# Second block's two output gates in three passes from split slabs, queries' norm applied in the logits' copies, recurrence gates and short keys moved up

## Chip, core and metric

One core of a Trainium2 chip runs the whole program, a stack of three model blocks on 256 tokens of width 1024, in one launch. The metric is the device time of one execution in microseconds (us). Each core has a matrix engine (TensorE; in rows PE for its matmuls, PEld for its weight loads, clock 1.2 or 2.4 GHz), VectorE (DVE), ScalarE (ACT), GpSimd (POOL) and SyncE (SP), which issues the large loads. Matmul results land in eight PSUM banks. Each engine runs its own instructions in the order in which they are written and waits on semaphores for the others.

## What is computed

The change lies in the second block's mixer. Cut to it, with `s` = 256 tokens, 8 heads of 128, 2 key and value heads, 8 index heads of 64:

```python
xn = _rmsnorm(x, mix_norm); h = xn @ w_in          # w_in: 1024 x 6216
lru_x, lru_gate, q, k, v, qi, ki, wi, gate_a, gate_b = _split_cols(h)
ua = _causal_dwconv(lru_x, ...)                    # width 4
r = sigmoid(ua @ wa + ba); i = sigmoid(ua @ wx + bx)     # 8 blocks of 128
log_a = -8 * r * softplus(-lam); a = exp(log_a)
u = sqrt(-expm1(2 * log_a)) * (i * ua)
h_t = a_t * h_(t-1) + u_t                          # over the 256 tokens
ya = (h * gelu(lru_gate)) @ w_lru_br
qh = _rmsnorm(q per head, q_norm); kh = _rmsnorm(k per head, k_norm)
score = sum_h wi_h * relu(qi_h . ki / 8)           # causal; top 64 keys for each token
probs = softmax(qh . kh / sqrt(128) + bias[bucket(dist)])   # over these 64
yb = (probs @ v) @ w_attn_br
merged = sigmoid(gate_a) * ya + sigmoid(gate_b) * yb
x = x + merged @ w_out
```

The first block (a mixer and 16 experts) runs ahead of it, and this block's feed-forward part and a third block of two layers behind it. All is in float32.

## The kernel before

**Products.** The activations `h` of the second block stand feature-major (feature on the partition, 256 tokens along the row) in three forms: whole in `hT`, and as a rounded high part and the rest, `h2_high` and `h2_low`. `feature_major` (products at L1039) multiplies a whole float32 slab of weights by the whole activations. `feature_major3` splits each weight slab too: ACT's `high` (L1855) writes the rounded high part to a spare area, DVE's `low` (L2366) writes the rest over the slab, and `mm3` (L968, L969, L970) adds three products: high x high, high x low, low x high. A slab is 1024 x 512 weights, 2 MB; `high` and `low` work on it in two halves of 128 x 2048. A product of 128 x 256 has 32 places in a slab (4 groups of output features, 8 chunks of the 1024).

**Loads and banks.** Slabs go through a ring of three places. SP issues the load of a slab when TensorE has finished the slab three before it (`load`, L751). Results take the four work banks in turn (`open_bank`); TensorE may fill a bank only when the result that it held four batches before has been copied out, mostly by ACT (`copied`, `frees`).

**Order on TensorE around the change.** Slabs `lru_x`, `lru_x1`, `lru_gate`, `q`, `kv`; five sums of squares with `ones_mean` (`qk_ms`, L1367), four for the queries, one for the keys; slab `qi`; the recurrence's gates (`lru_ri`, L1376); the short keys and index weights (`kiwi`, L1380); slabs `gate_a` (whole, L1039); eight index score batches (`indexer`, L1400), two ahead of slab `gate_b` 0 and six within it; `gate_b` (whole); the logits (L1420); the slabs `lru_out` 0 and 1; transposes of the softmax (L1430 to L1432).

**Order on DVE.** `low` of `qi`; five reciprocals (L2771) and products (L2772) that norm queries and keys in place; the recurrence (L2778 to L2785, scan L2787) with ACT's tanh (L2024), exp (L2027) and square root (L2034) between; its product with the gelu gate in two parts (`u_high`, `u_low`, L2793 to L2796); the index scores (L2807, L2809), whose `relu` copies ACT makes; mask (L2816); eight rounds of maximum and replacement for tokens 0 to 127 (L2822, L2823); `low` of `lru_out` 0; eight rounds for tokens 128 to 255; threshold, bias and row maximum of the logits (L2829 to L2846); `low` of `lru_out` 1; the softmax's division. The order on each engine is written out by hand, and nothing reorders it.

## Time and profile before

| | us |
|---|---|
| median of three runs | 2667.01 |
| lowest, highest | 2665.62, 2667.71 |
| the profiled execution's own time | 2669.58 |
| its span, first to last instruction | 2667.8 |
| TensorE busy, share of the span | 2319.9, 87% |
| VectorE busy | 1345.1, 50% |
| ScalarE busy | 808.8, 30% |

The profile is of one execution. Its rows give times from the start of the span. TensorE's busy time counts overlapping matmuls once; how fast it goes is read from the distance of their starts. A row of the timeline merges neighbours of one line and shape and gives, in brackets, the idle time before it and who ended it. The stretch that the change touches begins at about 1190 us and ends at about 1376 us. What lies behind it is reached in the same order by both kernels.

### The profile page before, as it was taken

Reading aid. Unit: us, or ns where it says so; the run is one execution under the profiler, and the core shown is the slowest. Engines: PE = TensorE matmul, PEld = TensorE weight load, DVE = VectorE, ACT = ScalarE, POOL = GpSimd, SP = SyncE. Lnnn points to the kernel's source line nnn. Section 1 sums busy time; section 2 is a strip of 40 time slices with the busy share of each in tenths; the row PEclk is TensorE's granted clock in tenths of the full one; section 3 lists DMA queues with packets and bytes.
Section 4 is the critical chain, followed back from the end, with each engine's and each line's share of the span. In section 5 each row is a group of like instructions: output and inputs, shape, how many; then the busy total and the mean of one; then the engine's idle time right before and its main releaser. Section 6 shows DMA issues by size and latency. Waiting matters only on the chain.

```text
span 2667.8 us, 34798 instructions
## 1 busy us (share of the span) xinstructions
PE 2319.9 (87%) x14416; PEld 1695.4 (64%) x14416; DVE 1345.1 (50%) x1894; ACT 808.8 (30%) x1141; POOL 22.9 (1%) x41
## 2 busy tenths in 40 slices
PE   6999767666766676689999999999999999999999
PEld 5997222112211222149898998888968888887887
DVE  5865100000000000035687776877687778777776
ACT  3342000000000000024454334434574334345433
POOL 1000000000000000000000000000000000000000
PEclk9999887887788878899999999999999999999999
DMA  9948999999999999985445555555505555552553
GB/s 386 355 171 345 398 428 428 428 428 428 428 428 429 429 429 428 428 353 186 165 144 172 189 189 174 178 191 183 187 5 184 191 176 191 189 178 82 183 189 127
DMA packets 219734, 720.23 MB, mean 270 GB/s; under 512 B 8312, under 2 KB 126088, under 8 KB 191600
## 3 DMA queue, kind: packets, MB, share of 16 engines
q1 hardware_dynamic: 217632, 708.87, 68.6%
q0 software_dynamic: 2000, 9.91, 1.0%
q8 instruction: 75, 1.23, 0.2%
q14 instruction: 27, 0.22, 0.0%
HBM read 717.68 MB, written 3.16 MB: 270 GB/s over the span
## 4 chain that ended last, share of the span: by engine, by line
PE 64%; DMA 30%; DVE 3%; SPq 1%; issue 1%; ACT 1%; POOLq 0%; POOL 0%; DVEq 0%; ACTq 0%
PE bank L1494 12%; DMA AB<-in_w_up_e 8%; PE bank L968 6%; PE bank L1496 6%; PE bank L970 6%; PE bank L969 6%; DMA AB<-in_w_gate_e 5%; DMA AB<-in_w_down_e 5%; PE bank_pair L968 5%; PE bank_pair L969 5%; PE bank_pair L970 5%; DMA HT<-in_w_up_e 4%; DMA HT<-in_w_gate_e 3%; DMA HT<-in_w_down_e 3%; PE bank L1274 2%; PE bank L1039 2%
## 5 line engine op out<-in xcount | busy, mean ns | idle before, releaser
L1496 PEld LDWEIGHTS bank<-HT_r,ring_r 128*128 128x128 f32 x1408 | 265.3, 188 | 62.3
L2665 DVE TENSOR_TENSOR A<-bank,A 128x512 f32<-128x512 f32 x16 | 11.1, 692 | 580.6 <-PE bank L1274 580.6
L1496 PE MATMUL bank<-HT_r,ring_r 128*128 128x256 f32 x1408 | 277.3, 278 | 0.0
L970 PE MATMUL bank<-HT_r,ring_r 128*128 128x256 f32 x904 | 255.9, 283 | 0.0
L2366 DVE TENSOR_TENSOR ring_r<-ring,AB_r 128x2048 fp32r<-128x2048 f32 (+1 forms) x81 | 179.9, 2261 | 51.1 <-ACT AB_r L1855 50.0
L1494 PE MATMUL bank<-HT_r,AB_r 128*128 128x512 f32 x640 | 203.2, 399 | 2.2 <-DVE HT_r L2374 2.2
L1494 PE MATMUL bank<-HT_r,AC_r 128*128 128x512 f32 x640 | 201.0, 395 | 0.0
L2366 DVE TENSOR_TENSOR ring_r<-ring,AC_r 128x2048 fp32r<-128x2048 f32 x66 | 148.4, 2289 | 73.8 <-ACT AC_r L1855 73.7
L2366 DVE TENSOR_TENSOR ring_r<-ring,A_r 128x2048 fp32r<-128x2048 f32 (+1 forms) x80 | 171.6, 2179 | 27.1 <-ACT A_r L1855 27.1
L2092 ACT ACTIVATE XB<-XB 128x256 f32<-128x256 f32 x112 | 46.8, 418 | 436.4 <-DVE XB L2935 320.6
L1274 PE MATMUL bank<-ring,A 128*32 128x512 f32 x768 | 116.2, 732 | 70.6 <-DMA ring<-in_w_up_e 47.6
L969 PE MATMUL bank_pair<-ring_r,XA_r 128*128 128x512 f32 x448 | 174.5, 389 | 0.0
L970 PEld LDWEIGHTS bank<-HT_r,ring_r 128*128 128x128 f32 x904 | 173.5, 192 | 0.0
L1855 ACT ACTIVATE AB_r<-ring 128x2048 fp32r<-128x2048 f32 (+1 forms) x79 | 145.0, 1883 | 57.2 <-PE bank L970 15.9
L970 PE MATMUL bank_pair<-A_r,XB_r 128*128 128x512 f32 x408 | 158.8, 389 | 0.0
L1956 ACT ACTIVATE A<-bank 128x512 f32<-128x512 f32 x16 | 9.6, 597 | 489.4 <-PE bank L1274 489.4
L2407 DVE TENSOR_REDUCE XB<-bank 128x256 f32<-128x512 f32 x176 | 120.8, 686 | 62.4 <-PE bank L1496 62.4
L968 PE MATMUL bank_pair<-A_r,XA_r 128*128 128x512 f32 x384 | 149.6, 390 | 0.0
L1855 ACT ACTIVATE AC_r<-ring 128x2048 fp32r<-128x2048 f32 x66 | 123.2, 1915 | 84.7 <-DMA ring<-in_ffn_w_gu 74.0
L1855 ACT ACTIVATE A_r<-ring 128x2048 fp32r<-128x2048 f32 (+1 forms) x80 | 142.2, 1816 | 12.9 <-DMA ring<-in_w_out 11.4
L1814 ACT ACTIVATE A<-bank 128x256 f32<-128x256 f32 (+2 forms) x56 | 22.7, 413 | 400.7 <-PE bank L1283 298.1
L969 PE MATMUL bank<-HT_r,AB_r 128*128 128x256 f32 x488 | 138.1, 283 | 0.0
(579 smaller groups left out, 4697.1 us busy)
## 6 DMA issues: line engine op xcount, KB each, us to landing
ring<-in_ffn_w_gu SPq DMA_DIRECT2D x88, 1024.0 KB, 6.7
ring<-in_w_gate_e SPq DMA_DIRECT2D x24, 2048.0 KB, 35.8
ring<-in_w_up_e SPq DMA_DIRECT2D x24, 2048.0 KB, 32.2
ring<-in_w_in SPq DMA_DIRECT2D x46, 1024.0 KB, 10.2
ring<-in_w_down_e SPq DMA_DIRECT2D x23, 2048.0 KB, 36.9
ring<-in_ffn_w_down SPq DMA_DIRECT2D x40, 1024.0 KB, 6.2
ring<-in_w_up SPq DMA_DIRECT2D x24, 1024.0 KB, 6.6
A<-in_w_ada SPq DMA_DIRECT2D x17, 1024.0 KB, 11.6
```

Source lines behind the costliest of these rows:

```text
L968: mm(out_, lhs[0], rhs[0], start=start, stop=False, skip_group_check=True)
L969: mm(out_, lhs[0], rhs[1], start=False, stop=False, skip_group_check=True)
L970: return mm(out_, lhs[1], rhs[0], start=False, stop=stop, skip_group_check=True)
L1039: last = mm(b[:, f * T:(f + 1) * T], w[:, at:at + P], src[:, k, :], start=(k == 0), stop=(k == n_k - 1))
L1274: last = mm(b[32 * j:32 * j + 32, :], xe_now[:, k, :], w[:, col0:col0 + 512], start=(k == 0), stop=(k == DC - 1), tile_position=(0, 32 * j ...
L1494: mm(both, high, h_both[:, :, k, :], start=(k == 0), stop=False, skip_group_check=True)
L1496: last = mm(both[:, 1, :], lows[k - k0], h_high[:, k, :], start=False, stop=(k == DC - 1), skip_group_check=True)
L1814: frees(run(dst, work_bank(name, i)[0:rows_, 0:n], ACT.Copy, scale=scale), name, i)
L1855: run(area[:, :], w[:, at:at + area.shape[1]], ACT.Copy).then_inc(S["high_ready"], 1)
L2092: run(f_act[b % 2], f_conv[b % 2], fn).then_inc(S["gelu_done"], 1)
L2366: v.tensor_tensor(twins[f"ring{slot}"][:, part], ring[slot][:, part], area[:, :].bitcast(fp32), ALU.subtract).then_inc(S["low_ready"], 1)
L2407: frees(v.tensor_reduce(dst, both, AX.X, ALU.add), name, i)
```

## The change

Both gates' slabs are loaded as two halves of 256 output features each and go through `high`, `low` and `mm3`, one half (one work bank, two groups of features) at a time. `high_half` on ACT and `low(..., which=...)` on DVE are placed one by one among the other work. The areas for the high halves are ones that are free at that point: a half's area is reused when the batches that read it are done. For the queries, 16 products with one column of `ones_mean` give the mean squares of each token and head as a column; `q_scale` is their root's reciprocal times 1/sqrt(128), and ACT multiplies by it when it copies the logits (16 copies of one head instead of 8 of two). Both norms' gains go into the keys (`gain_qk`). `kiwi` and `lru_ri` stand ahead of `qi` on TensorE, and the slab of `lru_ri` ahead of that of `qi` in the ring. The bias for the later tokens is loaded as two halves into other places, straight after the table that it is read from. `u_high` lies elsewhere.

```diff
@@ -253,14 +253,14 @@
     p.add("lru_gate", "WWWW", [1, 3], split=2)
     p.add("q", "WWWW", [1, 3], split=2)
     p.add("kv", "WW", [1], split=1)
-    p.add("qk_ms", "W" * 5)
+    p.add("qk_ms", "WW")
+    p.add("kiwi", "W")
+    p.add("lru_ri", "W" * 8, [7])
     p.add("qi", "WW", [1], split=1)
-    p.add("lru_ri", "W" * 8, [7])
-    p.add("kiwi", "W")
-    p.add("gate_a", "WWWW", [1, 3])
+    p.add("gate_a", "WWWW", [1, 3], split=2)
     p.add("wi", "W")
     p.add("score", "AA")
-    p.add("gate_b", "AAWAAAAWWW", [7, 9])
+    p.add("gate_b", "AAWAAAAWWW", [7, 9], split=2)
     p.add("logits2", "W" * 8)
...
-    bias2_last = AB[:, 2048:4096].rearrange("p (h s) -> p h s", h=8)
+    bias2_last = [a.rearrange("p (h s) -> p h s", h=4)
+                  for a in (const("dft_seq"), row("gate_f"))]
+    q_scale, gain_qk = narrow(16), narrow(1)
     bias_row = A[3][0:8, 1024:1536]
     relu_s = [A[6][:, at:at + 512].rearrange("p (d s) -> p d s", d=2) for at in (0, 512)]
     score = A[6][:, 1024:1536].rearrange("p (t s) -> p t s", t=TT)
...
     h_high, h_low = h_both[:, 0, :, :], h_both[:, 1, :, :]
-    u_high, u_low = fm(twins["AB"][:, 0:2048]), fm(twins["AC"][:, 0:2048])
+    u_high, u_low = fm(twins["HT"][:, 2048:4096]), fm(twins["AC"][:, 0:2048])
     h2_high, h2_low = fm(twins["AB"][:, 0:2048]), fm(twins["AB"][:, 2048:4096])
     hid_high = twins["A8"][:, 0:1536].rearrange("p (f t) -> p f t", t=T)
     hid_low = twins["A0"][:, 0:1536].rearrange("p (f t) -> p f t", t=T)
...
         t_ = {n: twins[n][:, :] for n in ("AB", "A3", "A4", "A5", "A6", "A8")}
-        if name in ("lru_x1", "lru_gate", "q", "kv", "qi"):
+        xn_r = twins["xn"][:, :, :].rearrange("p t d -> p (t d)")
+        if name == "qi":
+            return [(0, xn_r), (2048, t_["A6"])]
+        if name in ("gate_a", "gate_b"):
+            ht, a0 = twins["HT"][:, 2048:4096], twins["A0"][:, :]
+            a, b = {("gate_a", 0): (ht, xn_r), ("gate_a", 1): (t_["A6"], t_["A4"]),
+                    ("gate_b", 0): (a0, xn_r), ("gate_b", 1): (t_["A4"], xn_r)}[name, s]
+            return [(0, a), (2048, b)]
+        if name in ("lru_x1", "lru_gate", "q", "kv"):
             if (plan.split0[name] + s - plan.split0["lru_x1"]) % 2 == 0:
                 return [(0, twins["AC"][:, 2048:4096]), (2048, t_["A4"])]
             return [(0, t_["A3"]), (2048, twins["xn"][:, :, :].rearrange("p t d -> p (t d)"))]
         if name in ("lru_out", "attn_out"):
-            xn_r = twins["xn"][:, :, :].rearrange("p t d -> p (t d)")
             ht_0, ht_1 = twins["HT"][:, 0:2048], twins["HT"][:, 2048:4096]
...
@@ -866,13 +875,15 @@
         dense("lru_gate", w_in2, 2, 1024)
         dense("q", w_in2, 2, 2048)
         dense("kv", w_in2, 1, 3072)
-        dense("qi", w_in2, 1, 3584)
         sl = slot("lru_ri", 0)
         gate_w = [dram(n).rearrange("(b c) d -> c b d", c=P) for n in ("lru_wa_2", "lru_wx_2")]
         load("lru_ri", 0, [(ring[sl][:, i * D:(i + 1) * D].rearrange("p (b d) -> p b d", b=8), gate_w[i])
                            for i in range(2)])
-        dense("gate_a", w_in2, 2, 4168)
-        dense("gate_b", w_in2, 2, 5192)
+        dense("qi", w_in2, 1, 3584)
+        for name, c0 in (("gate_a", 4168), ("gate_b", 5192)):
+            for s in range(2):
+                dst = ring[slot(name, s)][:, :].rearrange("p (a k n) -> p a k n", a=2, k=8)
+                load(name, s, [(dst[:, a, :, :], k_rows(w_in2, c0 + 512 * s + 256 * a, 256)) for a in range(2)])
...
-        for i in range(5):
-            b = open_bank("qk_ms", i)
-            src = sq2[:, 2 * i:2 * i + 2, :].rearrange("p c t -> p (c t)") if i < 4 else sqk[:, :]
-            batch(mm(b[:, :], ones_mean[:, :], src, start=True, stop=True))
-        feature_major3("qi", 0, 0, h2_parts)
+        b = open_bank("qk_ms", 0)
+        for t in range(TT):
+            for h in range(8):
+                last = mm(b[:, 8 * t + h:8 * t + h + 1], sq2[:, h, t * P:(t + 1) * P], ones_mean[:, 0:1],
+                          start=True, stop=True)
+        batch(last)
+        b = open_bank("qk_ms", 1)
+        batch(mm(b[:, :], ones_mean[:, :], sqk[:, :], start=True, stop=True))
+        b = open_bank("kiwi", 0)
+        for k in range(DC):
+            last = mm(b[0:72, 0:T], w_kiwi[:, k, :], hT[:, k, :], start=(k == 0), stop=(k == DC - 1))
+        batch(last)
         pe.wait_ge(S["ua_ready"], 1)
         w = slab("lru_ri", 0)
         for i in range(8):
@@ -1375,12 +1393,25 @@
                 at = (i // 4) * D + n * P
                 last = mm(b[:, j * T:(j + 1) * T], w[:, at:at + P], l_ua[:, n, :], start=True, stop=True)
             batch(last)
-        b = open_bank("kiwi", 0)
-        for k in range(DC):
-            last = mm(b[0:72, 0:T], w_kiwi[:, k, :], hT[:, k, :], start=(k == 0), stop=(k == DC - 1))
-        batch(last)
+        feature_major3("qi", 0, 0, h2_parts)
+
+        def gate3_slab(name, s, batches, behind=None):
+
+            w = split_slab(name, s)
+            for g in range(2):
+                b = open_bank(name, batches[g])
+                for f in range(2):
+                    for k in range(DC):
+                        last = mm3(b[:, f * T:(f + 1) * T], w(2048 * g + 256 * k + f * P, P), h2_parts(k),
+                                   k == 0, k == DC - 1)
+                    if behind and f == 0:
+                        behind(2 * g)
+                batch(last)
+                if behind:
+                    behind(2 * g + 1)
+
         for s in range(2):
-            feature_major("gate_a", 2 * s, s, hT, DC)
+            gate3_slab("gate_a", s, (2 * s, 2 * s + 1))
         copied(pe, "kiwi", 0)
         b = open_bank("wi", 0)
         for t in range(TT):
@@ -1409,9 +1440,9 @@
 
         indexer(0)
         indexer(1)
-        feature_major("gate_b", 0, 0, hT, DC, behind=indexer_pair, batches=GATE_B_AT[0:2])
-        feature_major("gate_b", 0, 1, hT, DC, batches=GATE_B_AT[2:4])
-        pe.wait_ge(S["qk_ready"], 5)
+        gate3_slab("gate_b", 0, GATE_B_AT[0:2], behind=indexer_pair)
+        gate3_slab("gate_b", 1, GATE_B_AT[2:4])
+        pe.wait_ge(S["qk_ready"], 2)
         for t in range(TT):
...
+            w = loaded(act, name, s)
+            at, area = halves(name, s)[half]
+            run(area[:, :], w[:, at:at + area.shape[1]], ACT.Copy).then_inc(S["high_ready"], 1)
+
         filled(act, "kv", 0)
         run(k2[:, :, :].rearrange("p g t -> p (g t)"), work_bank("kv", 0)[:, :], ACT.Copy)
         frees(run(sqk[:, :], work_bank("kv", 0)[:, :], ACT.Square), "kv", 0)
         copy_out("kv", 1, v2[:, :, :].rearrange("p t n -> p (t n)"))
 
-        for i in range(5):
-            filled(act, "qk_ms", i)
-            frees(run(root[i][:, :], work_bank("qk_ms", i)[:, :], ACT.Sqrt, bias=eps_col[:, 0:1]), "qk_ms", i)
+        high_half("qi", 0, 0)
+        filled(act, "qk_ms", 0)
+        frees(run(q_scale, work_bank("qk_ms", 0)[:, 0:16], ACT.Sqrt, bias=eps_col[:, 0:1]), "qk_ms", 0)
+        filled(act, "qk_ms", 1)
+        frees(run(root_k[:, :], work_bank("qk_ms", 1)[:, :], ACT.Sqrt, bias=eps_col[:, 0:1]), "qk_ms", 1)
+        high_half("qi", 0, 1)
+        filled(act, "kiwi", 0)
+        for d in range(2):
+            run(ki[64 * d:64 * d + 64, :], work_bank("kiwi", 0)[0:64, 0:T], ACT.Copy)
+        frees(run(wi_rows, work_bank("kiwi", 0)[64:72, 0:T], ACT.Copy), "kiwi", 0)
+        high_half("gate_a", 0, 0)
 
         def ri(i):
 
@@ -2013,8 +2057,6 @@
             two("lru_ri", i, lambda f, b: run(dst[:, 2 * (i % 4) + f, :], b, ACT.Sigmoid,
                                               bias=col(bias, 2 * (i % 4) + f)))
 
-        for i in range(2):
-            copy_out("qi", i, qi[:, 2 * i:2 * i + 2, :].rearrange("p g t -> p (g t)"))
         for i in range(8):
             ri(i)
         for i in range(4):
...
-            run(ki[64 * d:64 * d + 64, :], work_bank("kiwi", 0)[0:64, 0:T], ACT.Copy)
-        frees(run(wi_rows, work_bank("kiwi", 0)[64:72, 0:T], ACT.Copy), "kiwi", 0)
+        for i in range(2):
+            copy_out("qi", i, qi[:, 2 * i:2 * i + 2, :].rearrange("p g t -> p (g t)"))
+        high_half("gate_a", 0, 1)
+        high_half("gate_a", 1, 0)
         act.wait_ge(S["mult_in"], 1)
         run(l_t[:, :, :], l_t[:, :, :], ACT.Sqrt).then_inc(S["mult_out"], 1)
+        high_half("gate_a", 1, 1)
         act.wait_ge(S["scan_done"], 1)
+        high_half("gate_b", 0, 0)
         for i in range(4):
             filled(act, "gate_a", i)
             frees(run(l_a[:, 2 * i:2 * i + 2, :].rearrange("p g t -> p (g t)"), work_bank("gate_a", i)[:, :],
                       ACT.Sigmoid), "gate_a", i)
+            if i == 1:
+                high_half("gate_b", 0, 1)
```

Left out are lines on views and areas, the logits' copies on ACT (described above), POOL's two loads of the bias in place of one, and the placement of `low` on DVE, which the pieces below and this list give: `qi` half 0 ahead of the roots' reciprocals, `qi` half 1 and `gate_a` 0 half 0 behind them; `gate_a` 0 half 1 behind the product that ACT's square root waits for; both halves of `gate_a` 1 ahead of the scan; `gate_b` 0 half 0 behind the scan's first product with the gelu gate, half 1 behind `u_low`; `gate_b` 1 half 0 between the fourth and fifth index score, half 1 behind the eighth.

**ScalarE from the values' copy to the first sigmoid of the recurrence.** Before (L1814 the values' copy and the copies of `qi`, L2008 the roots, L2013 the sigmoids):

```order
L1814 ACTIVATE A<-bank 128x512 [waits products_done]
L2008 ACT_TABLE_LOAD
L2008 ACTIVATE XA<-bank,eps_col 128x512 [waits products_done] x4
L2008 ACTIVATE XB<-bank,eps_col 128x512 [waits products_done]
L1814 ACTIVATE A<-bank 128x512 [waits products_done] x2
L2013 ACT_TABLE_LOAD
L2013 ACTIVATE AC<-bank,cols 128x256 [waits products_done]
```

Now (L1845 the values' copy, L2035 a high half, L2044 and L2046 the roots, L2050 and L2051 the short keys, L2057 the sigmoids):

```order
L1845 ACTIVATE A<-bank 128x512 [waits products_done]
L2035 ACTIVATE XA_r<-ring 128x2048 [waits slab_loaded0]
L2044 ACT_TABLE_LOAD
L2044 ACTIVATE small<-bank,eps_col 128x16 [waits products_done]
L2046 ACTIVATE XB<-bank,eps_col 128x512 [waits products_done]
L2035 ACTIVATE A_r<-ring 128x2048 [waits slab_loaded0]
L2050 ACTIVATE XB<-bank 64x256 [waits products_done]
L2050 ACTIVATE XB<-bank 64x256
L2051 ACTIVATE XB<-bank 8x256
L2035 ACTIVATE HT_r<-ring 128x2048 [waits slab_loaded1]
L2057 ACT_TABLE_LOAD
L2057 ACTIVATE AC<-bank,cols 128x256 [waits products_done]
```

Both halves of `qi` and the first of `gate_a` stand ahead of the first sigmoid; the copies of `qi` have gone behind the recurrence's exp.

**VectorE at the end of the index scores.** Before:

```order
L2809 SCALAR_TENSOR_TENSOR A<-A,small 128x256 [waits relu_done,relu_used]
L2809 SCALAR_TENSOR_TENSOR A<-A,small 128x256 [waits dve_own]
L2816 TENSOR_TENSOR A<-A,masks 128x128 [waits relu_used]
L2816 TENSOR_TENSOR A<-A,masks 128x256
L2822 MAX small<-A 128x8 [waits dve_own]
```

Now:

```order
L2874 SCALAR_TENSOR_TENSOR A<-A,small 128x256 [waits relu_done,relu_used]
L2874 SCALAR_TENSOR_TENSOR A<-A,small 128x256 [waits dve_own]
L2420 TENSOR_TENSOR ring_r<-ring,XA_r 128x2048 [waits high_ready,relu_used]
L2882 TENSOR_TENSOR A<-A,masks 128x128
L2882 TENSOR_TENSOR A<-A,masks 128x256
L2888 MAX small<-A 128x8 [waits dve_own]
```

The last low half of `gate_b` stands between the scores and the mask, and it waits for ACT's high half.

**ScalarE from the sixth to eighth index score to the logits' copies.** Now (L2094 relu, L2035 a high half, L2106 the sigmoids of `gate_b`, L2115 the logits' copies):

```order
L2094 ACTIVATE A<-bank_pair 128x512 [waits relu_used,products_done] x4
L2035 ACTIVATE XA_r<-ring 128x2048 [waits slab_loaded1,products_done]
L2106 ACTIVATE A<-bank 128x512 [waits products_done] x2
L2035 ACTIVATE XB_r<-ring 128x2048 [waits slab_loaded2]
L2106 ACTIVATE A<-bank 128x512 [waits products_done] x2
L2035 ACTIVATE XA_r<-ring 128x2048 [waits slab_loaded2]
L2115 ACTIVATE A<-bank,small 128x128 [waits products_done,qk_ready]
```

Before, both halves of `lru_out` 0 stood between the second and the third sigmoid. Now the second of them stands behind the fourth, and the first L2035 row, the last half of `gate_b`, waits until TensorE has done with slab `gate_b` 0, whose high half lay in the same area.

## Rows read from the trace of the kernel before

**Rows 1.** Chain that ended last: start us, us, what; 1281 to 1366

```profile
1286.07 27.63 PE bank L1039 x128
...
1328.22 0.61 ACT A L2048
...
1331.00 0.64 DVE A L2816 x2
...
1337.40 4.49 DVE ring_r L2366 x2
1341.89 0.35 DVE small L2822
...
1361.46 4.41 DVE ring_r L2366 x2
...
1365.92 0.39 PE bank L968
```

**Rows 2.** Timeline of TensorE: start us, us, engine, line, operation, count, idle before

```profile
1190.18 0.47 PE L968 MATMUL bank<-AB_r,AC_r 128*128 128x256 f32 x1
...
1259.74 3.60 PE L1367 MATMUL bank<-A,ones_mean 128*128 128x512 f32 x8
...
1275.54 7.07 PE L1376 MATMUL bank<-AC,ring 128*128 128x256 f32 x32
1282.45 3.62 PE L1380 MATMUL bank<-HT,w_kiwi 128*72 128x256 f32 x16
1285.90 27.79 PE L1039 MATMUL bank<-HT,ring 128*128 128x256 f32 x128
1313.62 0.61 PE L1387 MATMUL bank<-consts,XB 8*128 8x8 f32 x4
...
1345.90 5.40 PE L1420 MATMUL bank<-A,HT 128*128 128x128 f32 x32
...
1350.95 0.47 PE L968 MATMUL bank<-AB_r,XA_r 128*128 128x256 f32 x1
...
1363.71 0.39 PE L968 MATMUL bank<-AB_r,HT_r 128*128 128x256 f32 x1 [0.91 <-DVE ring_r L2366]
...
1365.92 0.39 PE L968 MATMUL bank<-AB_r,HT_r 128*128 128x256 f32 x1 [0.50 <-DVE ring_r L2366]
```

**Rows 3.** Timeline of TensorE, 20 to 36 us: a restart, narrow products

```profile
20.57 8.04 PE L1103 MATMUL bank<-ones 128*128 128x512 f32 x12 [20.57 <-DVE XB L2423]
...
32.02 3.63 PE L1113 MATMUL bank<-ones,XB 128*128 128x1 f32 x32
```

**Rows 4.** Timeline of ScalarE, 1249 to 1298 us

```profile
1249.39 1.92 ACT L1855 ACTIVATE AC_r<-ring 128x2048 fp32r<-128x2048 f32 x1
1251.20 1.91 ACT L1855 ACTIVATE A_r<-ring 128x2048 fp32r<-128x2048 f32 x1
...
1276.36 1.28 ACT L2013 ACT_TABLE_LOAD   x1
1277.65 3.03 ACT L2013 ACTIVATE AC<-bank,cols 128x256 f32<-128x256 f32 x8
...
1283.38 3.38 ACT L2024 ACTIVATE XB<-AC,small 128x256 f32<-128x256 f32 x8
```

**Rows 5.** Timeline of VectorE, 1266 to 1316 us

```profile
1266.62 3.35 DVE L2771 RECIPROCAL XA<-XA 128x512 f32<-128x512 f32 x1
1270.01 0.75 DVE L2772 SCALAR_TENSOR_TENSOR HT<-HT,cols,XA 128x512 f32<-128x512 f32 x1
...
1300.40 4.77 DVE L2787 TENSOR_TENSOR_SCAN AC<-AC,A 128x256 f32<-128x256 f32 x8
...
1315.19 0.29 DVE L2807 TENSOR_SCALAR A<-A,small 128x128 f32<-128x128 f32 x1 [3.17 <-ACT A L2048]
```

**Rows 6.** Windows: us, busy PE, PEld, DVE, ACT, POOL, PEclk, DMA share, GB/s

```profile
1939.50:1942.20 2.70, 0.06 (x1) 0.00 (x0) 2.56 (x8) 0.00 (x0) 0.00 (x0) 1.00 0.00 0
...
1945.00:1946.00 1.00, 1.00 (x8) 0.39 (x4) 0.84 (x4) 1.00 (x6) 0.00 (x0) 0.50 0.00 0
```

## What was predicted

> **What bounds the kernel now.** I read the chain of waits first, then each engine's timeline in the stretch that is changed. The chain [rows 1] runs through TensorE while it works on `gate_a` (128 matmul records in 27.63 us) and through the index scores up to 1328; then it leaves TensorE: ACT's relu, DVE's mask at 1331.00, its rounds of maximum and replacement, `low` of `lru_out` 0 among them at 1337.40, and `low` of `lru_out` 1 at 1361.46. TensorE comes back at 1365.92. The reader is to see in [rows 2] that TensorE has work without a gap up to 1363.71 and then waits 0.91 and 0.50 us for DVE: from the scores on, DVE ends last, and TensorE is only 1.4 us less late. So time taken from TensorE ahead of `lru_out` 1 comes through only as far as it brings DVE's scores forward, and each microsecond that DVE gains or loses between 1331 and 1366 is one of the kernel.
>
> **Price on TensorE.** Six slabs in three passes take from 1190.18 to 1259.74, 11.6 us each; the two whole slabs of `gate_a` take from 1285.90 to 1313.62, 13.9 us each [rows 2]. Four slabs gain 4 x 2.3 = 9.1 us. The queries' sums: 16 narrow products have the form of the 32 records in 3.63 us [rows 3], against 8 of the 10 records up to 1263.2, 3.4 us: nothing. The logits' count is the same. So at most 9 us are there.
>
> **Price on the others.** A high half costs ACT 1.8 us from start to start [rows 4], a low half DVE 2.2 us (4.49 for two) [rows 1]; eight of each are added, 14.5 and 17.6 us. DVE loses four reciprocals and four products, 4 x 4.1 = 16.4 us [rows 5], but ahead of the recurrence, while seven of the eight low halves stand behind the recurrence's exp. I follow the three engines from 1259.7, each operation with its length in these rows.
>
> *Up to the recurrence.* TensorE: 3.5 for the queries, 0.8 for the keys, 3.4 for `kiwi` (1282.45 to 1285.90) [rows 2]: the recurrence's gates begin at 1267.5 instead of 1275.54. They need four work banks; the fifth batch waits for ACT's first sigmoid. ACT has in front of that sigmoid three high halves, the copies of roots and short keys and two table loads of 1.28 [rows 4]: values' copy to 1260.5, high half 1262.3, table 1263.6, roots 1264.8, high half 1266.6, short keys (they are ready at 1267.6) 1268.9, high half 1270.7, table 1272.0. TensorE stands from 1271.0 to 1272.8 and ends the gates at 1276.3, `qi` at 1287.9.
>
> *Recurrence.* Sigmoids to 1278.1 (before 1283.4), tanh 3.1, table 1.3, exp 3.3: 1285.8; two operations of 2.3 on DVE: 1290.4. ACT must first wait for `qi`'s second batch at 1287.9, copy it and make two high halves, so the square root ends at 1295.4 instead of 1298.0. DVE: product 2.3, two low halves 4.4, scan 4.8 [rows 5]: 1306.9, where before it was 1305.2. The five microseconds won at the sigmoids are gone. TensorE gets the low halves of `gate_a` just in time (one wait of 0.6 for the third half) and ends `gate_a` at 1311.7 (before 1313.6).
>
> *Scores.* DVE: `u_high`, low, product, `u_low`, low, 5 x 2.2: first score at 1318.0 instead of 1315.19 [rows 5]. TensorE runs `gate_b` 0 with six score batches between 1312.8 and 1327.5, 11.6 + 2.4 for the scores + 0.6 for waits. Four scores of 0.8, a low half 2.2, four of 1.0 and a wait of 0.7 end DVE's scores at 1328.0; the mask began at 1331.00 before [rows 1]: 3 us ahead.
>
> *The two new waits.* Now the last low half of `gate_b` stands ahead of the mask. ACT can make its high half only when TensorE has done `gate_b` 0, 1327.5 + 1.9 = 1329.4; DVE then needs 2.3: mask at 1331.7. Behind DVE's waiting instruction the mask, all rounds and `low` of both `lru_out` slabs are queued. The same sum made for the kernel before gives 1330.6 where the row says 1331.0, so I count the difference of sums, +1.1. The second: `low` of `lru_out` 0 half 1. ACT makes its high half behind the last sigmoid of `gate_b`, at 1339.1 + 0.5 + 1.9 = 1341.5; DVE would be there at 1340.3: +1.3. The bias added as two operations for the later tokens: +0.15. Small hand-overs that the sums miss by some tenths for each round trip between TensorE and ACT: +0.15. Together DVE hands over `low` of `lru_out` 1 **2.7 us later**. Without either wait it would be 0.2 us earlier; with `gate_b` ending 1 us later than I put it, 3.7 later. These are the bounds.
>
> *What becomes of TensorE's gain.* The logits go from 1338.9 to 1345.6 (ACT begins to copy them at 1341.5, a wait of 1.5; they were at 1345.90 to 1350.95) [rows 2], `lru_out` 0 ends at 1357.3, and then TensorE stands until about 1366: 8.5 us, the 9 us that it was to gain.
>
> *The clock.* An idle stretch of 2.7 us [rows 6] is followed by a granted clock of 0.50, which is 1.2 GHz, in the third microsecond of work behind it. After 20.57 us of idle 12 records of 128x512 take 8.04 us [rows 3], where such a record takes 0.43 at full clock (twice the 27.63 / 128 of a record of 256 columns) [rows 1]: 2.9 us lost. So behind 8.5 us of idle `lru_out` 1 begins at half clock. Nearest rows: 2.9 lost at the most, nothing at the least (the slab behind the waits of 0.91 and 0.50 shows no loss); of what is lost 0.6 lies in the wait for the second low half, which TensorE no longer reaches early. I take 1.5, in the upper half, as both idle rows show the drop. The Trainium skill ("TensorE: Matmul & The Clock Gate", Part 1) says that the throttled clock is the default and that activity releases it. By that rule work after a long wait always pays; the trace agrees [rows 3, 6].
>
> *Strict order.* DVE does no instruction ahead of one that waits; the chain in [rows 1] shows its rounds and `low` strictly in written order. The Trainium skill ("TensorE: Matmul & The Clock Gate", Architectural detail) says that ScalarE and VectorE are strict FIFO, while TensorE may pull weight loads ahead. It speaks against this change: if DVE could pass the waiting low half, the sum would be 1.1 less.
>
> *Moved and hidden.* The bias for the later tokens is loaded ahead of the queries' slabs instead of behind `qi`; its reader stands behind the threshold, far later in both. `lru_ri` and `qi` change places in the ring; each has over 10 us to land. Slabs of the gates are released later than needed by none: high halves are asked for more than 6 us after each release. If `gate_a` 0 lands after 1268.9, ACT's sigmoids go with it, microsecond for microsecond. 16 logits' copies instead of 8 cost ACT some 1.4 us more; they are done at 1346.8, and DVE asks for them at 1352.8.
>
> **Sum.** +2.7 + 1.5 = +4.2 us. The profiled execution took 2669.58 and would take 2673.8. It lies 2.6 above the median of the runs shown, so the median goes from 2667.0 to **2671.2**.
>
> **Rivals.**
>
> *The clock falls twice (slower than 0.2%).* TensorE also stands 1.8 us at the fifth gate batch. If the clock falls there too, up to 1.7 us are lost in `qi`; the high halves that wait for `qi` and `gate_b` shift by it, and both new waits grow. At a shift of 1.3 the time is 2671.2 + 1.3 = 2672.5; from 1.2 on it is over the bound. For it: [rows 6] fell after 2.7. Against it: no loss behind the 0.91 [rows 2], and nothing in between is measured in dense work. A clock loss of 2.9 instead of 1.5 gives the same.
>
> *The waits don't bind (no change).* If ACT's high halves come earlier than summed, DVE is 0.2 early, TensorE idles 6, and the clock costs 1.5: 2668.3.
>
> *The gain arrives (faster).* If DVE had slack that the chain hides, the 9.1 us would show: 2658. Against it stand the two waits for DVE in [rows 2].
>
> **How the numbers follow.** The forecast has 0.53, the clock twice or longer 0.27, no binding waits 0.13, the full gain 0.07. A change under 0.2%, 5.3 us, can't be told from none here. Faster needs under 2661.7: 0.07. Slower needs over 2672.3: 0.27. The same: 0.66. For 8 in 10 the range leaves out the full gain and the far end of the clock: 2665.5 (DVE 0.2 early, no clock loss, runs 1 us apart) to 2674.5 (3.7 + 2.9 + 0.9 for the runs).
>
> **What the changed profile would show.** TensorE idle for 8 to 9 us ahead of `lru_out` 1, ended by DVE; a granted clock of half for some microseconds behind it; DVE waiting about 1 us for ACT ahead of the last `gate_b` half and of the second `lru_out` 0 half; `gate_a` ending near 1311.7, the mask near 1332, transposes of the softmax some 4 us after 1376. I am wrong if DVE reaches the mask before 1330, or if TensorE's wait ahead of `lru_out` 1 is under 4 us.

## The result, and the profile after

| | before | after |
|---|---|---|
| median of 17 runs each, us | 2668.07 | 2675.32 |
| lowest, highest | 2664.16, 2670.17 | 2665.94, 2677.14 |
| span of the profiled execution | 2667.8 | 2675.3 |

The ratio is 1.0026, with a 95% interval from 1.002 to 1.0032: the changed kernel is slower by 0.26%, some 7 us. The forecast was 2671.2 and its range ended at 2674.5, so both were too low.

The page of the changed kernel, busy time of each engine:

```profile
PE 2331.0 (87%) x14568; PEld 1704.1 (64%) x14568; DVE 1347.8 (50%) x1898; ACT 822.9 (31%) x1154; POOL 23.5 (1%) x42
```

TensorE is busy for 11 us more than before, though four slabs now take 11.6 us instead of 13.9. All of it lies in the experts, ahead of the changed part (568.6 us busy between 300 and 1150, before 555.9), where the loads set the time: the sum of busy time says nothing on this change. TensorE's timeline in the changed kernel (start, us, engine, line, operation, count, idle time before and who ended it); it answers to [rows 2]:

```profile
1189.72 0.47 PE L979 MATMUL bank<-AB_r,AC_r 128*128 128x256 f32 x1
...
1259.27 4.26 PE L1378 MATMUL bank<-ones_mean,A 128*128 128x1 f32 x32
1263.38 2.05 PE L1382 MATMUL bank<-XB,ones_mean 128*128 128x512 f32 x2
1265.23 5.44 PE L1385 MATMUL bank<-HT,w_kiwi 128*72 128x256 f32 x16
1270.51 3.62 PE L1394 MATMUL bank<-AC,ring 128*128 128x256 f32 x16
1276.00 1.78 PE L1394 MATMUL bank<-AC,ring 128*128 128x256 f32 x7 [1.87 <-ACT AC L2057]
...
1315.10 0.61 PE L1418 MATMUL bank<-consts,XB 8*128 8x8 f32 x4
...
1345.91 3.72 PE L1451 MATMUL bank<-A,HT 128*128 128x256 f32 x16 [1.21 <-ACT A L2115]
...
1369.55 0.58 PE L979 MATMUL bank<-HT_r,AB_r 128*128 128x256 f32 x1 [8.42 <-DVE ring_r L2420]
...
1383.42 0.27 PE L1461 MATMUL bank<-consts,A 128*128 128x128 f32 x1
```

The wait of 8.42 us ahead of `lru_out` 1 is there, as forecast. Two rows are not as forecast: the short keys' 16 records take 5.44 us where they took 3.62 [rows 2], and the 32 narrow records take 4.26 where 32 of that form took 3.63 [rows 3]. No idle time stands ahead of either. The windows say why (us, busy time of PE, PEld, DVE, ACT, POOL, then the granted clock, DMA share, GB/s). Kernel before:

```profile
1262.50:1268.90 6.40, 6.40 (x45) 5.45 (x45) 6.30 (x3) 2.42 (x5) 0.00 (x0) 1.00 0.73 274
```

Changed kernel:

```profile
1262.50:1268.90 6.40, 6.40 (x16) 3.79 (x17) 4.79 (x5) 3.42 (x4) 0.00 (x0) 0.50 0.76 248
...
1361.10:1364.50 3.40, 0.03 (x1) 0.00 (x0) 3.37 (x3) 2.51 (x14) 0.00 (x0) 1.00 0.61 183
1364.50:1369.50 5.00, 0.00 (x0) 0.00 (x0) 4.97 (x4) 2.17 (x9) 0.00 (x0) 0.50 0.78 295
1369.50:1374.60 5.10, 5.05 (x23) 5.05 (x24) 5.03 (x5) 5.10 (x10) 0.00 (x0) 0.50 0.02 3
```

The clock was granted at half (1.2 GHz) twice. The second time is behind the long wait, from 1364.5 to 1374.7. The first time TensorE was busy without a gap: the clock fell at 1262.1, 2.8 us after the narrow sums began, and stayed at half for 6.8 us, through the keys' sum and most of the short keys.

VectorE in the changed kernel, the halves ahead of the mask and of `lru_out`:

```profile
1321.39 0.28 DVE L2872 TENSOR_SCALAR A<-A,small 128x128 f32<-128x128 f32 x1
...
1333.82 2.29 DVE L2420 TENSOR_TENSOR ring_r<-ring,XA_r 128x2048 fp32r<-128x2048 f32 x1 [2.40 <-ACT XA_r L2035]
1336.03 0.62 DVE L2882 TENSOR_TENSOR A<-A,masks 128x128 f32<-128x128 f32 x2
...
1345.38 2.29 DVE L2420 TENSOR_TENSOR ring_r<-ring,XA_r 128x2048 fp32r<-128x2048 f32 x1 [0.66 <-ACT XA_r L2035]
...
1367.21 2.28 DVE L2420 TENSOR_TENSOR ring_r<-ring,AB_r 128x2048 fp32r<-128x2048 f32 x1
```

ScalarE, the high half for which the mask waits; TensorE's end of `gate_b` 0 lets it start:

```profile
1331.43 1.91 ACT L2035 ACTIVATE XA_r<-ring 128x2048 fp32r<-128x2048 f32 x1 [1.40 <-PE bank L981]
```

**Measuring by the stretch.** The first product in three passes behind the experts begins at 1190.18 before and at 1189.72 after; over all profiles of this study it begins anywhere from 1183.4 to 1190.2, and what follows the transposes takes 1287.8 to 1293.2 (one run apart, below). These differences lie outside the changed part. So kernels are compared by the time from that first product to the first transposes of the softmax, "the stretch": 185.91 us before, 193.70 after, +7.79. The rest takes 1291.7 before and 1291.9 after. The stretch falls into four pieces:

| piece | forecast | measured |
|---|---|---|
| end of `gate_a` on TensorE | -1.9 | +1.94 (123.44 to 125.38) |
| from there to the mask on DVE | +3.0 | +3.55 (17.38 to 20.93) |
| from there to `low` of `lru_out` 1 | +1.6 | +0.80 (30.38 to 31.18) |
| from there to the transposes (clock) | +1.5 | +1.50 (14.71 to 16.21) |
| sum | +4.2 | +7.79 |

### The profile page after: what moved, and what is told of

Same layout as the page of the kernel before. It is cut to its first block, busy times and chain, and to the rows that moved or that the text cites. A ratio compares the mean times of both kernels' runs of the same rounds, so it can differ in the third digit from the quotient of the medians.

```text
span 2675.3 us, 35104 instructions
## 1 busy us (share of the span) xinstructions
PE 2331.0 (87%) x14568; PEld 1704.1 (64%) x14568; DVE 1347.8 (50%) x1898; ACT 822.9 (31%) x1154; POOL 23.5 (1%) x42
## 4 chain that ended last, share of the span: by engine, by line
PE 63%; DMA 31%; DVE 3%; ACT 1%; SPq 1%; issue 1%; POOLq 0%; POOL 0%; DVEq 0%; ACTq 0%
PE bank L1525 12%; DMA AB<-in_w_up_e 11%; DMA AB<-in_w_gate_e 9%; DMA AB<-in_w_down_e 9%; PE bank L979 7%; PE bank L980 7%; PE bank L981 7%; PE bank L1527 6%; PE bank_pair L979 5%; PE bank_pair L980 5%; PE bank_pair L981 5%; PE bank L1285 2%; PE bank L1320 1%; DMA A<-in_w_ada 1%; SPq L760 1%
## 5 line engine op out<-in xcount | busy, mean ns | idle before, releaser
L1527 PEld LDWEIGHTS bank<-HT_r,ring_r 128*128 128x128 f32 x1408 | 265.3, 188 | 62.4
L1527 PE MATMUL bank<-HT_r,ring_r 128*128 128x256 f32 x1408 | 277.3, 278 | 0.0
L981 PE MATMUL bank<-HT_r,ring_r 128*128 128x256 f32 x968 | 274.8, 284 | 0.0
L2420 DVE TENSOR_TENSOR ring_r<-ring,A_r 128x2048 fp32r<-128x2048 f32 (+1 forms) x83 | 178.4, 2183 | 28.3 <-ACT A_r L1886 27.5
L981 PEld LDWEIGHTS bank<-HT_r,ring_r 128*128 128x128 f32 x968 | 186.8, 193 | 0.0
L2420 DVE TENSOR_TENSOR ring_r<-ring,AC_r 128x2048 fp32r<-128x2048 f32 x65 | 146.2, 2288 | 69.5 <-ACT AC_r L1886 69.4
L1845 ACT ACTIVATE A<-bank 128x256 f32<-128x256 f32 (+2 forms) x56 | 22.9, 413 | 392.5 <-PE bank L1294 295.6
## 6 DMA issues: line engine op xcount, KB each, us to landing
A<-in_w_ada SPq DMA_DIRECT2D x17, 1024.0 KB, 11.6
```

Of the source, the lines that this page charges most:

```text
L981: return mm(out_, lhs[1], rhs[0], start=False, stop=stop, skip_group_check=True)
L1527: last = mm(both[:, 1, :], lows[k - k0], h_high[:, k, :], start=False, stop=(k == DC - 1), skip_group_check=True)
L2420: v.tensor_tensor(twins[f"ring{slot}"][:, part], ring[slot][:, part], area[:, :].bitcast(fp32), ALU.subtract).then_inc(S["low_ready"], 1)
```

## The experiments

All kernels in one table. `gate_a` ends and stretch are of one profiled execution each; the last two columns are of the timed runs, each group of kernels with runs of the kernel before on the same chip. The edits below are given in short form. "At half behind the sums": whether the clock was granted at half in the 15 us from 69.5 us on in the stretch.

| kernel | at half behind the sums | `gate_a` ends | stretch | median | ratio to before, interval |
|---|---|---|---|---|---|
| before | no | 123.44 | 185.91 | | |
| after | yes | 125.38 | 193.70 | 2675.32 | 1.0026 (1.002 to 1.0032) |
| after_again | yes | 125.38 | 193.79 | 2672.46 | 1.0023 (1.0009 to 1.0037) |
| a1_wide_sums | yes | 125.39 | 193.70 | 2670.97 | 1.0009 (0.9999 to 1.0019) |
| a5_interleaved | no | 126.18 | 194.24 | 2674.12 | 1.0032 (1.0022 to 1.0042) |
| a6_sums_wide_as_before | no | 121.90 | 190.35 | 2672.45 | 1.0017 (1.0008 to 1.0025) |
| a7_sums128 | no | 122.05 | 190.49 | 2670.08 | 1.0009 (1.0 to 1.0018) |
| a2_filler | yes | 125.39 | 192.22 | 2673.71 | 1.0013 (1.0003 to 1.0023) |
| a4_mask_first | yes | 125.39 | 193.53 | 2671.09 | 1.0022 (1.0013 to 1.0031) |
| b1_gate_b_whole | no | 122.05 | 194.01 | 2675.09 | 1.0032 (1.0021 to 1.0043) |
| b2_gates_whole | yes | 127.12 | 200.03 | 2675.66 | 1.0037 (1.0024 to 1.005) |
| b4_gates_whole_early | yes | 127.13 | 189.66 | 2670.83 | 1.0012 (1.0004 to 1.0021) |
| b5_gate_b_whole_early | yes | 125.40 | 187.94 | 2666.70 | 0.9993 (0.9984 to 1.0002) |
| b3_gate_a_whole | yes | 127.15 | 194.79 | 2673.43 | 1.0024 (1.0015 to 1.0033) |
| b6_gate_b_whole_sums128 | no | 122.05 | 184.57 | 2664.92 | 0.9995 (0.9986 to 1.0004) |
| d1_before_plus_narrow | yes | 130.18 | 192.65 | 2673.52 | 1.0025 (1.0015 to 1.0035) |
| c6_best | no | 120.06 | 182.17 | 2670.43 | 1.0009 (1.0 to 1.0019) |
| c7_best | no | 120.10 | 180.37 | 2662.68 | 0.9989 (0.998 to 0.9998) |

The medians follow the stretch only roughly (a1 has the changed kernel's stretch to 0.01 us and a median 4 us lower), which is why a difference of 3 us is read from the stretch; its two profiles of the changed kernel differ by 0.1 us.

### Theory and rivals

After the two traces my theory was: the narrow sums let the clock fall (3.3 us), and `gate_b`'s halves put waits ahead of the mask and of `lru_out` (the rest). Rivals: something else drops the clock; the loss is `gate_a`'s; the recurrence's move or the norm itself carries it.

### The sums

a1_wide_sums:

```diff
-  last = mm(b[:, n:n + 1], sq2[...], ones_mean[:, 0:1], ...)
+  last = mm(b[:, 32 * n:32 * n + 32], sq2[...], ones_mean[:, 0:32], ...)
```

> The changed kernel with one edit: each of the 16 sums of the queries' squares multiplies 32 columns of ones in place of 1 (the sum stands 32 times in the bank, the copy reads every 32nd column). Theory A: the narrow sums let TensorE's clock fall. In the changed kernel it was granted 0.50 from 1262.5 to 1268.9, beginning 3 us into the sums and with no idle time ahead of it, where the kernel before shows 1.00; 6.4 us at half are 3.2 us lost, and every step behind is waited for, so they reach the end. Expected here: 1.00 throughout that stretch, the mask near 1332.8 instead of 1336.0, 2672.1 us. Rival B: something else lets the clock fall (the step from values to sums, or the four small batches): the half clock stays, 2675.3 us. Rival C: the clock stays up but the three microseconds are absorbed by ACT's high halves ahead of the sigmoids: mask at 1335 or later, 2675 us.

Its TensorE, sums and short keys:

```profile
1254.92 4.32 PE L1379 MATMUL bank<-ones_mean,A 128*128 128x32 f32 x32
...
1260.90 5.42 PE L1386 MATMUL bank<-HT,w_kiwi 128*72 128x256 f32 x16
```

Theory A missed: nothing changes, 32 columns aren't enough to tell the theories apart. The sums' real undoing, a6_sums_wide_as_before, takes the four wide products of the kernel before (the scale is then read from the wrong columns, so its logits are wrong and only its time counts):

```diff
-  for t in range(TT): for h in range(8): last = mm(b[:, 8*t+h:8*t+h+1], sq2[...], ones_mean[:, 0:1], ...)
+  for i in range(4): last = mm(b[:, :], ones_mean[:, :], sq2[:, 2*i:2*i+2, :], ...)
```

> The changed kernel with the queries' sums undone alone: four products of 128x512 as in the kernel before, in place of the 16 narrow ones; the scale is then read from the wrong columns, so the logits are scaled wrongly, and all else is as in the changed kernel. Theory A (the narrow sums let the clock fall): 1.00 behind the sums, 3.3 us from the clock and 0.9 from the sums themselves (3.4 instead of 4.3), of which the sums' part may end in ACT's high halves: transposes at 189.5 to 190.4 from the first product instead of 193.7; 2672. Rival B (the step to the whole products of the short keys lets it fall): half clock again, 193.

```profile
1259.08 3.59 PE L1377 MATMUL bank<-A,ones_mean 128*128 128x512 f32 x8
```

The clock stays, the stretch is 190.35: 3.35 less. Nearly the same comes from a7_sums128, which changes the width alone and keeps the sums right (each product writes 128 columns and the next begins one column on, so the bank ends with the 16 sums):

```diff
-  last = mm(b[:, 8*t+h:8*t+h+1], sq2[...], ones_mean[:, 0:1], ...)
+  last = mm(b[:, 8*t+h:8*t+h+128], sq2[...], ones_mean[:, 0:128], ...)
```

> The changed kernel with each of the 16 narrow sums multiplying 128 columns of ones in place of 1; the products are written one column further each time, so that the first column of each stays and the bank ends with the same 16 sums. Theory A (it is the narrow products in a row that let the clock fall; 32 columns were still too few, four products of 512 columns were not): 1.00 behind the sums, no longer than 4.3 us of sums, recurrence's gates at 77.3 from the first product instead of 80.79, gate_a ends at 121.9 to 122.1, transposes at 190.4 as in the run with the sums undone. Rival B (what counts is not the width but the kind of sum or its 16 small weight loads): half clock again, 193.7.

Its sums, its short keys and a window over them:

```profile
1259.01 3.74 PE L1378 MATMUL bank<-ones_mean,A 128*128 128x128 f32 x32
...
1263.45 3.62 PE L1385 MATMUL bank<-HT,w_kiwi 128*72 128x256 f32 x16
```

```profile
1262.00:1269.00 7.00, 7.00 (x35) 5.12 (x34) 6.93 (x7) 5.53 (x8) 0.20 (x1) 1.00 0.74 245
```

16 products of 128 columns take 3.74 us, 16 of one column 3.63 at full clock (b1, below): the width costs nothing here, and it keeps the clock.

a5_interleaved put each narrow sum behind one product of the values (for this TensorE's wait for the queries' copies moves ahead of the values too; no idle time stands there):

```diff
   for t in range(TT): for k in range(DC):
     last = mm3(b[...], h2_parts(...), w(...), ...)
+    summed = mm(sums[:, 8*t+k:8*t+k+1], sq2[...], ones_mean[:, 0:1], ...)
```

> The changed kernel with the queries' sums moved: each of the 16 narrow sums of one column stands behind one of the 16 products of the values (the second batch of kv) instead of all together behind them. All times from the first product in three passes behind the experts (189.72 us into the changed kernel's 1000s, 1190.18 in the kernel before), since that start differs by up to 5 us between runs: there the softmax's transposes begin at 193.70 in the changed kernel and at 185.91 in the kernel before. Theory A: 4.3 us of narrow sums in a row let the clock fall; among wide products they don't. Clock 1.00 up to lru_out 1, gate_a ends 3.3 us earlier (122.1 instead of 125.4), transposes at 190.4; in time 3.3 us less, 2672. Rival B: any narrow sums do it, or it falls with the recurrence's batches: half clock again, 193.7.

```profile
1275.14 1.30 PE L1392 MATMUL bank<-AC,ring 128*128 128x256 f32 x4 [3.76 <-ACT AC L2055]
```

The clock stays up behind the sums, as theory A said, but the values' batch ends later, ACT's queue with it, and TensorE waits 3.76 us instead of 1.87 at the fifth recurrence batch. Behind this wait the clock fell for 3.4 us, from 0.8 us into the work on. The gain is gone: 194.24. The wait of 1.87 to 1.89 there had no fall behind it in any of the ten profiles that show it.

The cause alone, in the kernel before (d1_before_plus_narrow):

```diff
+  if i == 4:
+      for n in range(16): mm(b[:, n:n + 1], sq2[...], ones_mean[:, 0:1], ...)
```

> The kernel before with the 16 narrow sums added and nothing else: they are multiplied behind its four wide sums, ahead of the keys' sum, and nobody reads them. The suspected cause alone. TensorE's work grows by 4.3 us, and up to the scores TensorE sets the time there. Theory A (narrow products in a row let the clock fall, also without any other part of the change): half clock for some 6 us behind them, 4.3 + 3.3 = 7.6 us later: gate_a ends at 131.0 from the first product instead of 123.44, transposes at 193.5 instead of 185.91. Rival B (it needs the short keys' products directly behind, which here come 19 us later): 1.00 throughout, 127.7 and 190.2.

Its narrow sums, and the window behind their start:

```profile
1261.09 4.67 PE L1369 MATMUL bank<-ones_mean,A 128*128 128x1 f32 x32
```

```profile
1263.40:1270.60 7.20, 7.20 (x30) 6.17 (x31) 7.13 (x5) 0.69 (x1) 0.00 (x0) 0.53 0.20 74
```

The stretch grows by 6.74, of which 3.63 is the work and 3.1 the clock (7.6 were forecast, with 4.3 us of work, which was the length at a fallen clock). Narrow sums do it alone. Of 11 profiled executions with the sums of 1 or 32 columns in a row, 10 show the fall. The other is b1:

```profile
1255.69 3.63 PE L1379 MATMUL bank<-ones_mean,A 128*128 128x1 f32 x32
...
1260.12 3.62 PE L1386 MATMUL bank<-HT,w_kiwi 128*72 128x256 f32 x16
```

b1 has the same narrow sums, keeps the clock, and ends `gate_a` at 122.05, as a7 does: so the 3.35 us are the clock's and not the work's. The fall isn't certain in each execution; the changed kernel's second profile, after_again, has it again.

The trace of the kernel before had shown such a fall, directly behind the 32 narrow records of [rows 3] that the prediction took its price from. The next row there, and a window over it:

```profile
35.51 4.52 PE L1103 MATMUL bank<-ones 128*128 128x512 f32 x6
```

```profile
36.20:39.50 3.30, 3.30 (x6) 1.22 (x5) 2.67 (x2) 3.30 (x8) 2.94 (x5) 0.50 1.08 434
```

Six records of 128x512 would take 2.6 us at full clock (0.43 each); they take 4.52, with no idle time ahead of them. In all 18 profiles the clock falls to half at this place, 2.9 to 4.4 us after the 32 narrow records began. Behind the groups of 16 narrow records (1.93 us each, near 97 and 147 us) it falls in none.

> The changed kernel once more, for its time beside the other runs of this call and for a second profile. Theory: again half clock for 6 to 7 us behind the narrow sums (six of the seven profiled kernels that have them in a row behind the values show it), again 8.4 us of idle TensorE ahead of lru_out 1, 193.7 from the first product to the transposes. Rival: the clock fall is a matter of chance and not there in half of the executions: 190.4.

### The wait ahead of `lru_out` 1

a2_filler:

```diff
   for s in range(2):
+      if s: b = open_bank("lru_out", 2); 8 x mm(b[:, :], ones_mean[:, :], k2[...], start=True, stop=True)
       feature_major3("lru_out", 2 * s, s, ...)
```

> The changed kernel with 8 whole products of 128x512 (0.86 us each by the sums' records, 6.9 us together) put between the two slabs of lru_out, into the bank that the second slab overwrites: TensorE has work of no use in its 8.4 us of waiting. It prices the clock behind that wait. Theory: the wait costs 2.5 us of clock (granted 0.50 from 1364.7 to 1374.6, of which 5 us with work); with the filler the clock stays 1.00, DVE's hand-over at 1369.5 doesn't move, the softmax's transposes begin at 1380.9 instead of 1383.4, 2672.8 us. Rival: the transposes are bound by DVE's softmax and not by TensorE's clock, or the clock falls all the same: 2675.3 us.

```profile
1360.51 7.03 PE L1459 MATMUL bank<-A,ones_mean 128*128 128x512 f32 x16
...
1369.09 0.39 PE L979 MATMUL bank<-HT_r,AB_r 128*128 128x256 f32 x1 [1.55 <-DVE ring_r L2424]
```

```profile
1369.40:1381.50 12.10, 11.60 (x97) 11.39 (x96) 11.79 (x10) 5.13 (x9) 0.00 (x0) 1.00 0.00 1
```

The clock stays at 1.00 and the stretch shrinks by 1.48, not 2.5: at full clock TensorE waits another 0.50 for the second low half, and the first product of the slab isn't waited for any less. Work of no use in a wait pays here, but it pays what the clock costs and no more.

### The gates

b1_gate_b_whole and b2_gates_whole multiply `gate_b`, or both, whole again (in b1 to b6 the whole slabs are multiplied by the high parts of the activations alone, since the whole activations are overwritten by then; the work is that of whole products):

```diff
-  gate3_slab("gate_b", 0, GATE_B_AT[0:2], behind=indexer_pair)
+  feature_major("gate_b", 0, 0, h2_high, DC, behind=indexer_pair, batches=GATE_B_AT[0:2])
-  high_half("gate_b", ...), low("gate_b", ...)          # all of them; b2: gate_a's too
```

> The changed kernel with gate_b undone: its two slabs are again multiplied whole, gate_a stays in three passes, and no half of gate_b is made (gate_b is computed from the high parts of the tokens, since the whole ones are overwritten by then; the time is that of whole products). Theory A: gate_b's split costs more than it gives, since its low halves stand ahead of the scores and the mask. Then the first score comes 4.4 us earlier on DVE and is paced by TensorE as before: mask at 1332.5, lru_out 1 handed over near 1365, no half clock behind it, transposes near 1377, 2669 us, though TensorE works 4.6 us more; the half clock from 1262.5 stays. Rival B: the waits lie with gate_a's halves and the clock alone: mask at 1336, 2675 us or more.

> The changed kernel with both gates multiplied whole again and none of their halves made; what is left of the change is the queries' norm in the logits' copies, the narrow sums, and the moved-up keys and recurrence gates (both gates are computed from the high parts of the tokens; the time is that of whole products). Theory A (the narrow sums cost 3.2 us of clock, the split halves the rest): clock 0.50 for 6 us behind the sums, no wait at the fifth recurrence batch, gate_a ends near 1317, the mask near 1334, no idle and no half clock ahead of lru_out 1, transposes near 1377.7, 2669.6 us. Rival B: the queries' norm and the order carry the loss: 2673 or more. Rival C: DVE's 16 us less give a gain: 2665 or less.

Both missed by far: 194.01 and 200.03. VectorE of b1:

```profile
1343.08 2.29 DVE L2414 TENSOR_TENSOR ring_r<-ring,XA_r 128x2048 fp32r<-128x2048 f32 x1 [8.85 <-ACT XA_r L2036]
```

I had left the second high half of `lru_out` 0 where the change puts it, behind the last sigmoid of `gate_b`, which whole slabs reach later. The undoing wasn't clean. b4_gates_whole_early and b5_gate_b_whole_early put it back:

```diff
+  high_half("lru_out", 0, 1)        # ahead of gate_b's third sigmoid, behind half (0, 0)
-  high_half("lru_out", 0, 1)        # behind the last sigmoid
```

> The run with both gates whole, and the second high half of lru_out 0 put back ahead of gate_b's third sigmoid, where its area is free as soon as no gate is split. In the run before it, that half stood behind the last sigmoid and DVE waited 8.84 us for it, so that run didn't show what the split halves cost. Both gates are computed from the high parts of the tokens. Theory A: without split halves no new wait is left; DVE hands over lru_out 1 near 175 from the first product (177.5 with the clock fall if it comes, less if not), the wait of TensorE ahead of it is under 2 us, transposes at 189.0 with the clock fall behind the sums and 185.7 without; 2671 or 2668. Rival B: moving the keys, the recurrence and the norm itself costs more: 192 or more.

> The changed kernel with gate_b whole and the second high half of lru_out 0 ahead of gate_b's third sigmoid (gate_b computed from the high parts of the tokens); gate_a stays in three passes. It tells the two gates apart: both whole gave 189.66 from the first product to the transposes, both split 193.70, with the clock fall behind the sums in both. Theory A (gate_b's split carries the loss, gate_a's is a small gain): gate_a ends at 125.4, the mask 17.4 behind it at 142.8, TensorE waits under 1.5 us ahead of lru_out 1, transposes at 187.9. Rival B (gate_a's split carries it, through the fifth batch and DVE's late scan): 190 or more. If the clock doesn't fall behind the sums, all numbers are 3.3 less.

TensorE of b5, `lru_out` 1:

```profile
1362.33 0.39 PE L980 MATMUL bank<-HT_r,AB_r 128*128 128x256 f32 x1 [0.98 <-DVE ring_r L2414]
```

> The changed kernel with gate_a whole and gate_b in three passes (gate_a computed from the high parts of the tokens). Theory A: the two waits that gate_b's halves bring stay (2.4 us ahead of the mask, 0.7 ahead of lru_out 0's second half) and with them 8.4 us of idle TensorE and the second clock fall; gate_a ends at 127.1 from the first product instead of 125.4, the mask begins at 147 and the transposes at 194.5. Rival B (gate_a's halves on ACT and DVE are what makes the scores late): the scores are paced by TensorE again, mask near 145, transposes near 191.

b3 is the mirror of b1, `gate_a` whole and `gate_b` split. All four, with the clock at half behind the sums in each:

| | `gate_b` whole | `gate_b` split |
|---|---|---|
| `gate_a` whole | 189.66 | 194.79 |
| `gate_a` split | 187.94 | 193.70 |

`gate_a`'s split gains 1.7 or 1.1 us. `gate_b`'s, with the late place that it forces on `lru_out` 0's second high half, costs 5.1 or 5.8, although it takes 4.6 us from TensorE: DVE's and ACT's halves stand exactly between scores and `lru_out`.

The two readings of each differ by the clock behind the long wait. In b3 it came back earlier than in the changed kernel, 3.6 us into `lru_out` 1 instead of 5.2:

```profile
1365.01 0.58 PE L980 MATMUL bank<-HT_r,AB_r 128*128 128x256 f32 x1 [8.41 <-DVE ring_r L2417]
```

```profile
1361.90:1368.60 6.70, 3.59 (x17) 3.59 (x18) 6.67 (x6) 5.81 (x18) 0.00 (x0) 0.50 0.27 99
```

Up to TensorE's first product of `lru_out` 1 the four kernels take 177.29 and 181.60 (`gate_a` whole), 175.57 and 179.83 (`gate_a` split). So by the waits alone `gate_a`'s split gains 1.7 or 1.8 and `gate_b`'s costs 4.3 both times. From that product to the transposes it is 12.4 us where the clock was kept, 13.2 in b3 and 13.9 in the changed kernel: another 0.8 or 1.5 that the long wait costs.

With the clock's 3.35 behind the sums taken off, both gates whole come to 186.3, near the 185.91 of before: the norm in the logits' copies and the moved keys and recurrence give or take 0.4 together, though DVE loses 16 us of work by them. That work lay where DVE waits anyway.

Does the wait ahead of the mask hold the rest? a4_mask_first:

```diff
-  low("gate_b", 1, which=(1,))      # ahead of the mask
+  if (t, r) == (0, 2): low("gate_b", 1, which=(1,))     # behind two rounds
```

> The changed kernel with DVE's last low half of gate_b moved behind the mask and the first two rounds of maximum and replacement, which need nothing of it: they fill the 2.40 us that DVE waits for ACT's high half there. Theory A (this wait is on the path): everything behind is 2.1 us earlier, transposes at 191.6 from the first product, 2673.2. Rival B (the second wait takes over: the second high half of lru_out 0 needs the area that gate_b's last half holds, so it comes behind the last sigmoid, at gate_b's end on TensorE, whatever DVE does): DVE waits 2.8 us there instead of 0.66, transposes at 193.0, 2674.7.

```profile
1341.18 2.29 DVE L2420 TENSOR_TENSOR ring_r<-ring,XA_r 128x2048 fp32r<-128x2048 f32 x1 [3.00 <-ACT XA_r L2035]
```

Rival B holds: the mask comes early, the 2.4 us are gone, and the second wait grows from 0.66 to 3.00. The stretch gains 0.17. Both waits hang on TensorE's progress in `gate_b`, and taking the first away feeds the second.

The two causes together, b6 (b5's edit and a7's):

> The run with gate_b whole (187.94 from the first product to the transposes, with the clock fall behind the sums), now with the sums over 128 columns as well: the two causes taken away together. If they add up, 187.94 - 3.35 = 184.6, which is 1.3 less than the kernel before (185.91) and 9.1 less than the changed kernel. If the scores, once TensorE is earlier, wait for the scan on DVE instead, 186 to 188. gate_b is computed from the high parts of the tokens.

184.57, as forecast to 0.03: the two add up (3.35 + 5.76 of the 9.13 us by which it is under the changed kernel), and what `gate_a`'s split gains is left over. It is 1.3 us less than before in the stretch; by time no difference can be told (0.9995, 0.9986 to 1.0004).

### A version that beats both

c6_best keeps all of the change and moves the halves:

```diff
+  sums over 128 columns (a7)
+  high_half("gate_a", 0, 0) behind the recurrence's sigmoids; its low behind DVE's first recurrence product
+  low("gate_a", 1, which=(0,)) ahead of dve.wait_ge(S["mult_out"], 1)
-  ("gate_b", 1): (A4, xn)   lru_out 0: (A0, xn)
+  ("gate_b", 1): (A4, A0)   lru_out 0: (xn, A0)      # gate_b's last high half while the scores run
+  low("lru_out", 0, which=(1,)) behind 2 rounds of the later tokens
+  low("lru_out", 1) ahead of threshold and bias
```

> A version meant to beat both: the changed kernel with (1) the sums over 128 columns, (2) gate_a's first high half behind the recurrence's sigmoids on ACT and its low half behind DVE's first recurrence product, (3) gate_a's third low half ahead of the product that waits for the square root, (4) gate_b's last high half in the area that gate_b's second slab needn't wait for (the one of its first half), so it can be made while the scores run, (5) lru_out 0's second low half behind two rounds of the later tokens, (6) lru_out 1's low halves ahead of the bias. From the first product, by the rows of the changed kernel: gate_a ends at 119.4 (125.38 less 3.35 of clock, 1.87 and 0.65 of waits), first score 126, mask 138 (was 146.3), softmax done on DVE at 179.6 and transposes at 179.7, 14 less than in the changed kernel and 6.2 less than in the kernel before: 2661 us. If DVE's total from mask to softmax is the bound (theory), TensorE still waits some 4 us ahead of the transposes and the clock falls there. Rival: the early lows take what they give, since DVE has no idle time left: transposes at 184 or more, 2666.

TensorE of c6, its second group of transposes:

```profile
1375.21 0.48 PE L1461 MATMUL bank<-consts,A 128*128 128x128 f32 x1 [4.04 <-DVE XB L2922]
```

The first transposes come at 182.17 (179.7 forecast; DVE waited 1.99 us for `lru_out` 0's second high half, and TensorE stood 4.55 us ahead of them). Then TensorE stands another 4.04 us: its banks are emptied by DVE's products of `gate_a` and `lru_out` (L2922), which stand behind the low halves of `attn_out` 0. What lies behind the first transposes takes 1298.3 instead of some 1292. The stretch as I measure it hid that; the median, 2670.43, didn't. c7_best takes this wait away:

```diff
+  for i in (2 * t, 2 * t + 1): gated_lru(i)       # inside the softmax's division, for t = 0 and 1
-  gated_lru(0); low("attn_out", 0); gated_lru(1..3)
+  low("attn_out", 0)
+  low("lru_out", 0, which=(1,)) behind 4 rounds instead of 2
```

> The version meant to beat both, with the two waits that its first form showed taken away: DVE's products that empty the banks of lru_out stand ahead of attn_out 0's low halves, two of them while ACT makes the exponentials of the later tokens (in the first form TensorE waited 4.04 us for them behind its first transposes, and ran them at half clock), and lru_out 0's second low half stands behind four rounds instead of two (it waited 1.99 us). Theory: DVE's total from mask to softmax is the bound; mask at 137.9 from the first product as in the first form, softmax done and transposes at 179.5, TensorE waits under 2 us ahead of them and the clock stays 1.00; 6.4 less than the kernel before: 2661 us. Rival: TensorE, idle while DVE does the softmax, lets the clock fall again and the value sums run at half clock: 2663.

```profile
1364.61 0.33 PE L1461 MATMUL bank<-consts,A 128*128 128x128 f32 x1 [2.71 <-DVE XA L2929]
```

```profile
1364.60:1368.50 3.90, 3.89 (x17) 3.70 (x18) 3.90 (x4) 2.72 (x5) 0.00 (x0) 0.56 1.05 402
```

180.37 (179.5 forecast), 5.5 less than before and 13.3 less than after; what follows takes 1293.2, 1.5 more than before. Median 2662.68 beside 2666.86 of before and 2672.46 of the changed kernel, on the same chip; ratio to before 0.9989 (0.998 to 0.9998). By the ratio the whole is some 3 us faster than before (0.5 to 5.3). So a kernel with both gates split, wide sums and the halves placed anew can be faster than the one before. How much of this is the gates' split isn't shown: `lru_out`'s low halves and DVE's products moved too, and these moves were not run with the gates whole. b6, which has `gate_b` whole and none of them, stands at 184.57. The rival's part holds too: behind a wait of 2.71 the clock falls to half for 3.4 us.

## Why the prediction was wrong, point by point

- **The step that failed** is in *Price on TensorE*: "The queries' sums: ... nothing." The work was priced right: 3.63 us in [rows 3] and 3.63 in b1. What the sum lacked is what these products do to the clock: 3.35 us at the end of `gate_a` (125.38 against 122.05 in a7), 3.35 in the stretch (193.70 against 190.35 in a6). It is nearly all of the miss of 3.6 in the stretch (7.79 against 4.2). [Rows 3] showed narrow products at full clock for 3.6 us; but the clock fell 0.5 us behind them, past the last row shown there, and I looked for clock falls behind idle time only.
- **The clock step** let the clock fall behind idle time alone. The Trainium skill ("TensorE: Matmul & The Clock Gate", Part 1) speaks of how busy the engine has been; by the profile's rows TensorE is busy for all of 1262.5 to 1268.9 and has half the clock. A busy row is not proof of a kept clock.
- **The rival "the clock falls twice"** had the right shape (two falls, slower than the bound) and the wrong place: it put the first fall behind the 1.8 us at the fifth batch. That wait is there (1.87 us, as summed), with the clock at 1.00 behind it. The fall came 13 us earlier and cost 3.35, not 1.3. The 1.7 us that this rival names as the most stand in no row. Its 2672.5 came nearer to 2675.32 than the forecast did, but not by its mechanism.
- **Clock behind the long wait**: right in kind. 8.42 us idle (8.5 forecast), half clock from 1364.5 to 1374.7, +1.50 in the sum (1.5 forecast), 1.48 in a2. That the size agrees to the hundredth is luck: 1.5 was a choice between 0 and 2.9, and behind the same wait of 8.4 us the ten profiles that have it lose 0.5 (b1) to 1.6 us (a6), by when the clock fell and came back.
- **The waits**: right in kind and nearly in size. Mask piece +3.55 (+3.0), the piece behind it +0.80 (+1.6), since DVE waited 0.66 for `lru_out` 0's second half instead of 1.3. In a4 they stood in for each other, which the prediction's list of waits did not say.
- **`gate_a` ends at 1311.7, mask near 1332, transposes some 4 us after 1376**: 1315.10, 1336.03, 1383.42. Each holds the 3.35 us of clock, and with the 0.46 us by which the stretch began earlier they are 3.9, 4.8 and 3.9 late; with the sums wide, in a7, `gate_a` ends at 122.05 in the stretch, which is 1312.2 on the clock of before.
- **What becomes of TensorE's gain**: right. It stands idle ahead of `lru_out` 1.
- **The chances**: slower by over 0.2% had 0.27 and came true; "the same" had 0.66. The range ended at 3.7 + 2.9 + 0.9 above; the terms in it were priced, one was missing.
- **Small slips in the sums**, none of which changes the answer: the second wait is 1341.5 - 1340.3 = 1.2, not 1.3; TensorE from 1357.3 to 1366 is 8.7, not 8.5; the lower end, 0.2 and 1 under 2667.0, is 2665.8, not 2665.5.

## What to carry to other kernels

Ask of every small product that a change puts in a row on TensorE what it does to the clock, not only how long it takes; where the width is free, as 128 columns for one were here, write the wide form. Read the rows behind a priced row too. Before you split work from a busy engine over two others, see where on these two the pieces land: the same kind of split gained 1.7 to 1.8 us in a place with slack, and between two steps of the chain it cost 4.3, and 0.8 to 1.5 more by the clock behind the wait that it made. When a wait is taken away and nothing comes of it, look for the next one that hangs on the same event, and check the work behind your milestone too.

## What the runs showed of the hardware

- TensorE's clock fell to half 2.2 to 3.0 us after 16 narrow products (32 records, 1 or 32 columns) began, with no idle time ahead of the fall, and stayed there for 6.8 us, in 10 of 11 profiles. It did not with 128 or 512 columns (six profiles with such sums, the kernel before among them), nor with narrow products between wide ones (one).
- The same fall stands in all 18 profiles near 35 us, 2.9 to 4.4 us after the 32 one-column records of [rows 3] began, for 3.4 or 6.8 us. Behind 16 such records (1.93 us) there was none. Other products stood around each of these groups, so only the runs on the queries' sums tell the narrow ones apart as the cause.
- Sixteen products with 128 columns took 3.74 us, with one column 3.63, both at full clock.
- Behind idle time of 8.4 us (ten profiles) the clock had fallen 2.7 to 5.2 us into the wait and came back 2.9 to 5.5 us into the work. Behind 2.71 us (c7) it fell 0.4 us into the transposes and behind 3.76 us (a5) 0.8 us into the work, each time for 3.4 us. Behind 1.87 us no fall was seen.
- Why one execution of eleven kept its clock behind the sums, and how often the timed runs do, stays open: a profile shows one execution. The changed kernel's lowest run, 2665.94, and a1's lower median may be such cases, but no row shows it.
